# The last attention unit of a one-layer encoder step: three weight transposes leave TensorE for VectorE and a round trip through DRAM

## What is computed

```
h = rms_norm(x);  p = h @ w_in                     # 2048 x 7168
A: stick-breaking attention, 12 heads x 64, causal over the whole past
C: chunk-band attention,      8 heads x 64, own chunk and 8 before
B: sliding-window attention, 12 query heads / 4 key heads x 64,
   window 128, distance penalty, one learned sink per head
o = concat(o_A*silu(g_A), o_B*silu(g_B), o_C*silu(g_C)) @ w_out
y = x + rms_norm(o)                                # and new key/value caches
```

## Time and profile before

| | |
|---|---|
| Median of 3 runs | 1932.54 us (1932.3 to 1933.33) |
| The profiled execution | 1932.13 us, span 1930.4 us, TensorE clock granted 0.997 |
| PE busy | 1898.9 us, 98% |
| DVE, ACT, POOL busy | 1246.1, 679.8, 53.6 us |
| DMA moved | 301.07 MB, of 880408 packets 618504 under 512 B |

### The profile page before, as it was taken

How to read it: one execution, slowest core, us unless ns; L and a number is a source line. 1 busy time by engine, 2 the same in 40 slices (tenths; PEclk the granted TensorE clock), 3 DMA queues, 4 the chain that set the end, 5 groups by cost and what they waited for, 6 DMA issues and landing times.

```text
span 1930.4 us, 31333 instructions
## 1 busy us (share of the span) xinstructions
PE 1898.9 (98%) x12652; PEld 1757.0 (91%) x12652; DVE 1246.1 (65%) x2242; ACT 679.8 (35%) x1281; POOL 53.6 (3%) x119
## 2 busy tenths in 40 slices
PE   6999999999999999999999999999999999999997
PEld 5999999999999999999999999999999988888886
DVE  7368787887878778454444454355425566866878
ACT  7234334343334334122222222233213354344453
POOL 4000000000000000000000000000000000000131
PEclk9999999999999999999999999999999999999999
DMA  6456777776776777666657667465446657555396
GB/s 246 117 121 137 161 159 163 149 150 152 149 164 149 163 148 163 142 138 142 138 127 157 132 141 141 106 141 119 109 97 143 138 195 286 192 172 187 121 262 223
DMA packets 880408, 301.07 MB, mean 156 GB/s; under 512 B 618504, under 2 KB 845592, under 8 KB 878968
## 3 DMA queue, kind: packets, MB, share of 16 engines
q1 hardware_dynamic: 877192, 290.35, 61.8%
q0 software_dynamic: 3072, 8.73, 2.2%
HBM read 210.45 MB, written 96.20 MB: 159 GB/s over the span
## 4 chain that ended last, share of the span: by engine, by line
PE 87%; DVE 9%; ACT 1%; DMA 1%; issue 1%; POOL 0%; SPq 0%; DVEq 0%; ACTq 0%; POOLq 0%
PE ps L1230 21%; PE ps L1231 20%; PE ps L1232 20%; PE ps L1430 4%; PE ps L1432 4%; PE ps L1431 4%; PE ps L1322 3%; PE ps L1401 3%; PE ps L1372 2%; PE ps L1294 2%; DVE arena L1922 1%; DVE act_lo L1789 1%; DVE arena L1782 1%; PE ps L1427 1%; PE ps L1426 1%
## 5 line engine op out<-in xcount | busy, mean ns | idle before, releaser
L1230 PE MATMUL ps<-act_hi,w_hi 128*128 128x352 f32 x2688 | 878.2, 327 | 0.3 <-DVE arena L1822 0.2
L1232 PE MATMUL ps<-act_hi,w_lo 128*128 128x352 f32 x2688 | 863.4, 321 | 0.0
L1231 PE MATMUL ps<-act_lo,w_hi 128*128 128x352 f32 x2688 | 862.9, 321 | 0.0
L1230 PEld LDWEIGHTS ps<-act_hi,w_hi 128*128 128x128 f32 x2688 | 504.4, 188 | 19.3 <-issue 14.1
L1231 PEld LDWEIGHTS ps<-act_lo,w_hi 128*128 128x128 f32 x2688 | 505.5, 188 | 0.0
L1232 PEld LDWEIGHTS ps<-act_hi,w_lo 128*128 128x128 f32 x2688 | 504.4, 188 | 0.0
L1531 ACT ACTIVATE w_hi<-w_raw 128x512 fp32r<-128x512 f32 x224 | 139.3, 623 | 338.9 <-DMA w_raw<-in_w_in_dram 338.9
L1797 DVE TENSOR_TENSOR w_lo<-w_raw,w_hi 128x512 fp32r<-128x512 f32 x224 | 150.8, 674 | 57.3 <-ACT w_hi L1531 57.1
L1598 ACT ACTIVATE arena<-arena,small 128x257 f32<-128x257 f32 (+6 forms) x180 | 101.2, 565 | 208.6 <-DVE small L1960 208.6
L2148 DVE STREAM_TRANSPOSE arena<-arena 128x1024 f32<-128x1024 f32 (+4 forms) x100 | 132.6, 1326 | 37.3 <-ACT arena L1738 36.5
L1738 ACT ACTIVATE arena<-arena 128x1024 f32<-128x1024 f32 (+1 forms) x60 | 61.1, 1019 | 237.4 <-DVE arena L1934 237.4
(11 more groups left out here) (191 smaller groups left out, 2121.5 us busy)
## 6 DMA issues: line engine op xcount, KB each, us to landing
w_raw<-in_w_in_dram SPq DMA_DIRECT2D x176, 256.0 KB, 3.5
weight_scratch<-arena SPq DMA_DIRECT2D x216, 128.0 KB, 3.3
arena<-weight_scratch SPq DMA_DIRECT2D x54, 512.0 KB, 4.6
b_out<-in_w_out_dram SPq DMA_DIRECT2D x72, 256.0 KB, 3.4
w_raw<-in_w_out_dram SPq DMA_DIRECT2D x70, 256.0 KB, 2.8
w_raw<-in_w_in_dram SPq DMA_DIRECT2D x96, 128.0 KB, 3.0
weight_scratch<-arena SPq DMA_DIRECT2D x80, 132.0 KB, 4.0
arena<-weight_scratch SPq DMA_DIRECT2D x40, 256.0 KB, 3.3
```

Source lines behind the costliest of these rows:

```text
L1230: mm(bank(g, GN), wh, ah, start=(k == 0), stop=False)
L1231: mm(bank(g, GN), wh, al, start=False, stop=False)
L1232: last = mm(bank(g, GN), wl, ah, start=False, stop=(k == KT - 1))
```

## The change

`by_blocks` is true for steps 0, 1 and 2 of unit 15 as well. The due time of `load_weights` in that unit is set 1.9 after `part_weights` (2.6 in the other b units). The number of a `turn` on PE is counted 3 lower.

```
+LAST_BY_BLOCKS = 3
 def by_blocks(u, i):
-    return u + 1 < NU and (UNITS[u][0] == "a" or i + 1 < STEPS[UNITS[u][0]])
+    if u + 1 == NU:
+        return i < LAST_BY_BLOCKS
+    return UNITS[u][0] == "a" or i + 1 < STEPS[UNITS[u][0]]
...
-  plan += [(at, "part_weights", u, i), (at + (2.6 if u >= B0 else 4.0), "load_weights", u, i)]
+  plan += [(at, "part_weights", u, i), (at + (4.0 if u < B0 else 2.6 if u + 1 < NU else 1.9), "load_weights", u, i)]
...
-            return u - NA + 1 if u + 1 < NU else NU - NA + i
+            return u - NA + 1 if u + 1 < NU else NU - NA + i - LAST_BY_BLOCKS
```

## The result

The changed kernel takes 1947.74 us (median of 6 runs, 1946.77 to 1950.32), the kernel before 1932.87 us in the same series (6 runs, 1932.3 to 1933.33): ratio 1.0079, 95% interval 1.0069 to 1.009, slower by 14.9 us. The direction was forecast, the size was not: +6.7 us and 1939.2 were, with a range that ended at 1944. The profiled execution of after took 1947.65 us, span 1945.8, against 1932.13 and 1930.4. Lines after the changed functions stand 5 higher: L1012 is part, L1023 load, L1066 store_mixed, L1110 piece_out, L1127 load_mixed, L1327 scores, L1339 turn, L1406 values.

What follows compares the result with a forecast made beforehand. PE was taken to bound the kernel, without slack: -2.32 (turns) + 7.66 (waits for weights) + 1.4 (clock) = +6.7 us, so 1932.5 + 6.7 = 1939.2 us. The range was 1932.8 to 1944 us.

Steps and rivals of the forecast that it cites:

- The turns: On PE in unit 15, turns 0, 1 and 2 go, taking 2.32 us off the path, the whole possible gain.
- The extra block transposes on DVE: Three of 1.28 us each on DVE, taken as hidden, cost 0; without cover the third would cost 1.28 us.
- SP's three round trips in a row: On SP's queue, each part waits behind the load before; with full engines PE waits 7.66 us for weights.
- full DMA engines: Near load_mixed at tile 55's end, slower landings add 3, 1.5 and 0 us to parts 0, 1 and 2.
- Part 2: SP's last part and its load come when load_mixed 2 and 3 have mostly drained, so 0 us is added.
- Part 0: SP's first part, issued 1 us behind 2.1 MB of load_mixed, gets 3 us more, from a store_mixed's landing.
- The clock term: PE's granted clock falls after the second long wait: 1.7 less the 0.3 of the last wait, +1.4 us.
- In time: Rival: all three weights land before PE wants them and the turns are pure gain, 1930.2 us; chance 0.12.
- Light round trips: Rival: SP's chain binds but DMAs land as in unit 14, +0.9 us, 1933.4, up to 1936; chance 0.25.
- Keep jam: Rival: values 2 wait 1.4 us more for keep 0 on ACT behind late load_mixed, +8.1, 1940.6 us; chance 0.08.
- The estimate by the fit: For the weight DMAs, 2.0 us plus bytes over 436 GB/s: last weights near 1576 us, sum -2.3 us.

Runs made afterwards that it cites:

- long_runs: Changed kernel with unit 15's 12 part DMAs written as runs of 4224 bytes instead of 128, weights landing in wrong places: 1941.68 us, ratio 1.0049.
- part0_first: Changed kernel with load_mixed 0 and 1 issued right behind part 0 instead of ahead of it: 1947.09 us, ratio 1.008.
- loads_last: Changed kernel with load_mixed 0 to 3 issued only behind load 2, and what they fetch split after tile 55: 1950.39 us, ratio 1.0098.
- loads_on_pool: Changed kernel with load_mixed 0 to 3 issued by GpSimd's queue at the same due times: 1947.35 us, ratio 1.0077.
- pe_kept_busy: Changed kernel with 60 and 40 extra identity transposes on PE ahead of values 0 and 1: 1947.99 us, ratio 1.0084.
- one_step: Changed kernel with only step 0 of the last unit going through DRAM (LAST_BY_BLOCKS 1 instead of 3): 1939.12 us, ratio 1.0039.
- one_step_clean: Changed kernel with only step 0 through DRAM, load_mixed 0 and 1 behind its load, and left work moved later: 1933.95 us, ratio 1.0009.
- loads_behind_all: Changed kernel with load_mixed 0 and 1 behind part 1, 2 and 3 behind load 2, splitting in its old place: 1958.68 us, ratio 1.0137.
- parts_unread: Kernel before the change plus 12 part-like DMAs that nothing reads, issued by SP, which waits for their landing: 1940.45 us, ratio 1.0049.
- two_steps_spread: Changed kernel with two steps by blocks, load_mixed 0 behind part 0, 1 to 3 behind load 1, output's left work later: 1952.5 us, ratio 1.0103.
- parts_unread_pool: Kernel before the change plus twelve part DMAs that nothing reads, issued by GpSimd's queue with the landing waits there: 1932.43 us, ratio 1.0001.

## Why the prediction was right, and where it was wrong

**Right.** PE has no slack, and what is put into its queue is paid: the output product's delay of 14.9 us is the loss. The turns are gone, 2.32 us are gained. The extra block transposes on DVE cost PE nothing; all three waits for weights are released by DMAs. The chain that decides is the one named, SP's three round trips in a row, and only the last lateness counts.

**The step that failed** is the length of that chain: "From the start of part to the issue of its load is 6.72 us", "of which SP needs 3.40 to issue", with 3, 1.5 and 0 us more for full DMA engines. From part to load I had 9.72, 8.22 and 6.72 us; measured are 13.18, 7.03 and 12.35 (starts in SP's queue above). Between load and next part I had 0.96 twice, measured 1.10 and 1.75; from load 2 to its landing 3.7, measured 4.53. My sum is 30.28 us, the measured one 39.94, and 1556.23 + 39.94 is 1596.17, where values 2 run. PE wanted them at 1578.81 (1579.07 on this execution's clock), so they are 17.36 us late where I had 7.66; less 2.32 is 15.0, measured 14.9.

Two terms hold nearly all of the 9.7 us; part 1 was 1.2 shorter than I had it, the stretches between and the last landing 1.8 longer. Part 2 (+5.6): I wrote that part 2 and load 2 come when load_mixed 2 and 3 "have mostly drained: 0". But I had also worked out that the change pushes these two loads back, to near 1571.5; they went out at 1576.59, 2.7 us ahead of part 2. The two findings were never put together. Part 0 (+3.5): I took 3 us from the landing of a store_mixed. That row gives a landing, and what stretched here is the issue, 10.43 us for 3.40, which also holds SP for everything behind it: with the waits of the chain, load_mixed 2 and 3 went out 13 us later than before. Nor is the issue alone to blame: in long_runs it took 2.30 us and the same round trip still 11.57. A neighbour of 264 KB, issued 3 us behind the big loads, was too light a measure for a part issued right behind them.

That the big loads cause it is shown by part0_first (4.00 us without them ahead) and loads_last (3.9 to 4.4 for all three), that their queue does not matter by loads_on_pool, and that the 128-byte runs make it worse by 5.3 of the 14.9 us by long_runs. Why SP's issue of many short runs stalls when the DMA engines are full is not seen in any row, and stays open.

**The clock term**, +1.4 us, is 0 in this kernel. The clock does fall behind both long waits, but I placed the fall after the second wait, with 0.3 us of wait left to swallow it; the last wait is 2.07 us and takes it in. pe_kept_busy shows the zero for the first fall, the rows beside it for the second. As a kind of cost it is real: 2.55 us in one_step. Here it brought the forecast nearer to the measurement by luck: without it the sum is +5.3.

**The rivals.** In time, 1930.2: fallen. Light round trips, +0.9: the stretch is not light. As a price it holds for the first steps, since loads_last waits 0.19 and 0.31 us on its first two and one_step_clean not at all, but for three steps it is low: loads_last waits 5.1 us in all where this rival had 3.2. Keep jam: not in this kernel, where values 2 wait for a DMA; its mechanism shows when load_mixed moves further, in loads_behind_all at 11.6 us. The estimate by the fit in the Trainium skill, "DMA: Bandwidth & Descriptors", section "Anatomy of one DMA", -2.3 us, is not borne out: loads 0 and 2 landed 3.4 to 4.1 us after their issue and load 1, behind load_mixed 2 and 3, 9.4 to 10.2.

**What I left out** is the cost of a held SP that no weights are needed for. The prediction moved load_mixed 2 and 3 by 8 us and asked only whether keep suffers. Late pieces of w_out were not priced at all. parts_unread loses 9.0 us in these ways alone. It is no second term of the change's sum, since the waits for weights cover it, but it means that earlier weights do not give the time back where load_mixed and the pieces of w_out come late for them: two_steps_spread and loads_last wait only 2.7 and 5.1 us for weights and are slower than the change still.

## What to carry to other kernels

When DMAs are added to an issuing queue, cost their issue in the place where they will stand, not in a quiet one: ask what big transfer is in flight then, and work out again where the change itself moves that transfer. One queue with waits in it is a chain, so three round trips through DRAM are added up, and all that is due behind them comes later and is a cost by itself. Taking 2.3 us from the busiest engine pays only where the replacement's queue has room; here it had it for one step of three, and then no time was gained.

## What the runs showed of the hardware

SP took 3.40 us in a quiet stretch, 2.7 to 4.5 for the parts of unit 15 where no pair of load_mixed stood just ahead, and 8.5 to 11.2 behind 2.1 MB of load_mixed (the 11.16 in pe_kept_busy) to issue four DMAs of 132 KB in 128-byte runs, and 2.30 and 5.77 there when the runs had 4224 bytes; big loads issued by GpSimd slow it in the same way (8.65 us). The Trainium skill, "DMA: Bandwidth & Descriptors", section "Issuing engines are not separate DMA queues", calls the sequencer time that a second issuer saves usually small beside the DMA; here it was not: a part's issue took 10.43 of the 13.18 us from its start to its load, and parts_unread and parts_unread_pool lie 0.48% apart (1.0049 and 1.0001), though their packets differ too. GpSimd issued such a part in 3.2 to 3.3 us in all six places of the two runs that had it do so, and in parts_unread_pool with some 17 times fewer packets (768 against 12864).
